# Forget gate's sums added on VectorE from a spread copy, in place of 8-row products on TensorE

## The reference

```
log_f = log_sigmoid(f_logit + forget_bias)            # (256, 8)
F = cumsum(log_f, axis=tokens)
logits[h,t,s] = q[t,h] . k[s,h] / 8 + F[t,h] - F[s,h]   # s <= t, else -inf
y_fox = softmax(logits) @ v
```

## Time and profile before

| | |
|---|---|
| median of 3 runs | 1119.39 us (1117.60 to 1119.49) |
| profiled execution | 1122.45 us, its span 1120.7 us |
| TensorE matmul busy | 1097.0 us, 98% |
| VectorE busy | 755.1 us, 67% |
| ScalarE busy | 604.4 us, 54% |
| GpSimd busy | 51.5 us, 5% |
| mean granted TensorE clock | 0.985 |
| DMA | 187.13 MB, 47.6% of the 16 engines' span for the weight queue |

### The profile page before, as it was taken

How to read it: one execution, slowest core, us unless ns; L and a number is a source line. 1 busy time by engine, 2 the same in 40 slices (tenths; PEclk the granted TensorE clock), 3 DMA queues, 4 the chain that set the end, 5 groups by cost and what they waited for, 6 DMA issues and landing times.

```text
span 1120.7 us, 22403 instructions
## 1 busy us (share of the span) xinstructions
PE 1097.0 (98%) x8864; PEld 1055.8 (94%) x8864; DVE 755.1 (67%) x1114; ACT 604.4 (54%) x898; POOL 51.5 (5%) x64
## 2 busy tenths in 40 slices
PE   8999999999999999999999999999997999999998
PEld 7899899899999999999999998988887999999998
DVE  6888897647776665567666677556657776665566
ACT  5447745486565454555555444545756565454453
POOL 0000000001310000110000010000000210000010
PEclk9999999999999999999999999989888999999999
DMA  6345434335545554565555455533323455555563
GB/s 243 114 160 170 150 118 151 113 113 188 180 170 214 187 189 165 185 212 188 200 198 177 160 200 190 174 128 113 113 76 113 163 186 216 187 187 175 185 213 113
DMA packets 31869, 187.13 MB, mean 167 GB/s; under 512 B 3904, under 2 KB 7360, under 8 KB 14016
## 3 DMA queue, kind: packets, MB, share of 16 engines
q1 hardware_dynamic: 31808, 186.27, 47.6%
HBM read 184.42 MB, written 1.05 MB: 166 GB/s over the span
## 4 chain that ended last, share of the span: by engine, by line
PE 89%; DVE 5%; ACT 3%; issue 2%; POOL 0%; DVEq 0%; POOLq 0%
PE acc L601 81%; PE area_a L601 4%; PE area_t L601 4%; DVE wlo L1440 1%; PE area_t L868 1%; ACT he L1089 1%; ACT L1089 0%; ACT s_z L1089 0%; DVE s_after L1992 0%; ACT s_a L1089 0%; ACT whi L1089 0%; DVE pp L1476 0%; DVE tmp L1618 0%; ACT n2r L1089 0%; ACT gates L1089 0%
## 5 line engine op out<-in xcount | busy, mean ns | idle before, releaser
L601 PE MATMUL acc<-hs,whi 128*128 128x256 f32 x3600 | 633.2, 280 | 3.5 <-DVE wlo L1440 2.0
L601 PEld LDWEIGHTS acc<-hs,whi 128*128 128x128 f32 x3600 | 551.1, 190 | 8.7 <-issue 5.8
L601 PE MATMUL acc<-hs,wlo 128*128 128x256 f32 x1800 | 502.1, 279 | 0.0
L1089 ACT ACTIVATE whi<-raw 128x1024 fp32r<-128x1024 f32 (+2 forms) x378 | 357.3, 981 | 162.1 <-PE acc L601 137.5
L1440 DVE TENSOR_TENSOR wlo<-raw,whi 128x1024 fp32r<-128x1024 f32 (+3 forms) x258 | 271.5, 1094 | 104.0 <-ACT whi L1089 103.3
L601 PEld LDWEIGHTS acc<-hs,wlo 128*128 128x128 f32 x1800 | 341.0, 189 | 0.2
L601 PE MATMUL acc<-hid,whi 128*128 128x256 f32 x1056 | 180.7, 277 | 0.2 <-DVE wlo L1440 0.2
L601 PEld LDWEIGHTS acc<-hid,whi 128*128 128x128 f32 x1056 | 159.1, 188 | 0.4 <-DVE wlo L1440 0.4
L601 PE MATMUL acc<-hid,wlo 128*128 128x256 f32 x528 | 146.0, 277 | 0.0
L1527 DVE TENSOR_TENSOR wlo<-raw,whi 128x1024 fp32r<-128x1024 f32 x120 | 141.2, 1219 | 6.3 <-ACT whi L1089 6.3
L1540 DVE TENSOR_TENSOR hbuf<-acc,sbuf 128x256 f32<-128x256 f32 x66 | 28.0, 425 | 113.8 <-PE acc L601 109.9
(11 more groups left out here) (315 smaller groups left out, 1071.9 us busy)
## 6 DMA issues: line engine op xcount, KB each, us to landing
raw<-in_w_gu SPq DMA_DIRECT2D x66, 1024.0 KB, 4.8
raw<-in_w_dn SPq DMA_DIRECT2D x48, 704.0 KB, 4.0
raw<-in_w_up SPq DMA_DIRECT2D x10, 1024.0 KB, 4.8
raw<-in_w_gates1b SPq DMA_DIRECT2D x8, 1024.0 KB, 4.8
raw<-in_w_out SPq DMA_DIRECT2D x8, 1024.0 KB, 4.8
raw<-in_w_qk SPq DMA_DIRECT2D x8, 1024.0 KB, 4.8
raw<-in_w_gates SPq DMA_DIRECT2D x8, 1024.0 KB, 4.8
raw<-in_w_projT_b SPq DMA_DIRECT2D x7, 1024.0 KB, 4.8
```

The source lines that it names most:

```text
L601: return nc.tensor.matmul(out, w, m, start=start, stop=stop, skip_group_check=True)
L1089: return nc.scalar.activation(out, in_, f, **kw)
```

## The change

`negf` becomes -F without the factor 8. TensorE's 8-row products in the fox_s steps are gone, and with them its wait for `forget_sums` and its use of `C_SEL` there. GpSimd gets a new part, `spread_forget`: it waits for `forget_sums`, stores `negf` to a DRAM scratch, waits for that, reads each head's row back to all 128 partitions with a DMA of its own (`decay_of`, in the order of the score slots), waits for all eight, and adds the causal mask in four instructions, one for each head group and query tile (`fox_bias`). VectorE waits for the one of these it needs (`fox_biased`) and adds `fox_bias` where it added the mask. `decay_of` lies where `osplit2_sb` comes later, `fox_bias` where `mixed2` and `up2` come later.

```
+        decay_of = arena("decay_of", 12288, (FOX_H, T))
+        fox_bias = [arena(f"fox_bias{tt}", 14336 + P * FOX_H * tt, (FOX_H, P * (tt + 1))) for tt in range(NT)]
...
-                        pe.wait_ge(S("forget_sums"), 1)
...
-                        m = mm(dst, q[cols(h), h // 2, queries(tt)], k[cols(h), h // 2, 0:keys(tt)], True, not fox)
-                        if fox:
-                            m = mm(dst, con[0:FOX_H, C_SEL + P * h:C_SEL + P * h + P], negf[0:FOX_H, 0:keys(tt)],
-                                   False, True)
+                        m = mm(dst, q[cols(h), h // 2, queries(tt)], k[cols(h), h // 2, 0:keys(tt)], True, True)
...
-                    v.tensor_scalar(negf[h, :], fsum[h, :], -float(HD) ** 0.5, None, ALU.mult)\
+                    v.tensor_scalar(negf[h, :], fsum[h, :], -1.0, None, ALU.mult)\
...
                     dve.wait_ge(S("a_full"), TURN_A[name] + 1)
+                    dve.wait_ge(S("fox_biased"), NT * hg + tt + 1)
                     v.scalar_tensor_tensor(f_sc[:, :, 0:ks], area_a[:, :, 0:ks], float(HD) ** -0.5,
-                                           heads4(causal(tt, C_CM), ks), ALU.mult, ALU.add)\
+                                           fox_bias[tt][:, 4 * hg:4 * hg + 4, :], ALU.mult, ALU.add)\
...
+            rows = nc.dram_tensor("forget_rows", (FOX_H, T), F32).ap()
+
+            def spread_forget():
+
+                pool.wait_ge(S("forget_sums"), 1)
+                pool.dma_start(rows, negf[0:FOX_H, :]).then_inc(S("forget_out"), 16)
+                pool.wait_ge(S("forget_out"), 16)
+                for n in range(FOX_H):
+                    h = n // 4 * 4 + HEAD_OF_SLOT[n % 4]
+                    pool.dma_start(decay_of[:, n, :], rows[h].partition_broadcast(P)).then_inc(S("forget_spread"), 16)
+                pool.wait_ge(S("forget_spread"), 16 * FOX_H)
+                for hg in range(2):
+                    for tt in range(NT):
+                        h, ks = slice(4 * hg, 4 * hg + 4), keys(tt)
+                        nc.gpsimd.tensor_tensor(fox_bias[tt][:, h, :], decay_of[:, h, 0:ks],
+                                                heads4(causal(tt, C_CM), ks), ALU.add).then_inc(S("fox_biased"), 1)
+
             gated_sums(up1, mixed1, BLOCKS["up1"], 24, 0)
             sum_squares(0)
             sum_squares(1)
             sum_squares(2)
+            spread_forget()
             gated_sums(up2, mixed2, BLOCKS["up2"], 16, 24)
```

## The result

| | before | after |
|---|---|---|
| median | 1117.69 us (5 runs, 1116.93 to 1119.49) | 1106.44 us (5 runs, 1104.61 to 1107.68) |
| ratio | | 0.9889, 95% interval 0.9876 to 0.9903 |
| profiled execution, span | 1122.45, 1120.7 us | 1105.72, 1103.9 us |
| mean granted clock | 0.985 | 0.995 |

The change makes the kernel about 1.1% faster: 11.3 us between these medians. The two profiled executions differ by more, 16.8 us of span; what follows has to explain both numbers.

The account below looks back on a forecast made before the run. TensorE bounds the kernel, with three engines handing each other work in the stage. Queue shifts of -16.5 us plus 0.3 and 1.0 gave -15.2, so 1104.2 us from the 1119.39 median; own range 1101.5 to 1107.5, wider 1101 to 1110.5.

Parts of the forecast that it names:

- 1, sb_s00: TensorE's fox_s00 shortens to 0.65 us and the tile behind it to 5.6, so sb_s00 is reached 5.9 us earlier.
- 4, stick-breaking 01: VectorE, no longer held at fox_s10, starts stick-breaking after sb_s01's logarithm, at 780.9 instead of 791.15: shift -10.3 us.
- 6, fox_s11's sum: VectorE's 3.37 us wait for TensorE before fox_s11's sum goes, bringing the accumulated shift to -13.6 us.
- 7, sb_s11's first pass: ScalarE's 2.88 us wait before sb_s11 goes; shift -16.5 us, kept by everything that follows.
- term (e): New TensorE gaps lower the clock behind them; only losses behind 790.5 count: 1.0 us added, bounds 0 and 3.0.
- the rival of the clock falling in the new gaps: Waits lower the clock behind sb_t01 and once more near fox_s10: saving only 11.5 us, time 1107.9; chance 12%.
- (d): Four GpSimd sums, 9 us in all at about 731 to 740, slow VectorE's splits: 0.3 us added, bounds 0 and 4.0.
- Term (a): VectorE's sum reads fox_bias instead of the mask, with same operands and shape: nothing added.
- Term (b): Scratch store and eight broadcasts after forget_sums at 714.7 land at 730 to 733, before first use at 746.8: nothing added.
- Term (c): Broadcasts share DMA engines with weight loads, which may land up to 4.8 us late: nothing added, bounds 0 and 2 us.
- Only the products' own time goes: In the fox_s steps, 64-row products stay slow and the clock still falls: perhaps 8 us saved, 1111; chance 4%.
- The late spread: GpSimd's DMAs run serially, fox_bias comes at 780, 33 us behind first use, stalling VectorE and TensorE: 1136; chance 5%.

Follow-up runs that it names:

- the second trace: Changed kernel run and profiled once more with no edit: 1106.31 us beside 1118.35 for the kernel before, ratio 0.990, span 1106.8.

## Why the prediction was right, and where it was off

The forecast was 1104.2 us and faster; the median is 1106.44, in the range of 1101 to 1110.5. The mechanism went step by step as forecast. The shifts compare the first two traces, each counted from its own fox_s00, which starts 0.8 us earlier after.

| step | forecast | measured |
|---|---|---|
| 1, sb_s00 (757.64, 751.17) | -5.9 | -5.7 |
| 2, fox_s01's sum (775.32, 767.73) | -6.9 | -6.8 |
| 3, sb_s01's first pass (784.07, 774.59) | -8.6 | -8.7 |
| 4, stick-breaking 01 (791.15, 780.00) | -10.3 | -10.4 |
| 6, fox_s11's sum (824.35, 811.34) | -13.6 | -12.3 |
| 7, sb_s11's first pass (834.21, 818.20) | -16.5 | -15.3 |
| sb_t11 (849.26, 833.23) | -16.5 | -15.3 |

The 1.2 us that steps 6 and 7 fall short are term (e): transposes of sb_t01 at 1.97 instead of 1.09 and the tile behind at 6.16.

**Step 1's size.** The saving was forecast as 15.2 us and is 11.3 in medians. That the time is only 2.2 us off is partly luck: the three runs of before that I started from had a median 1.7 us above that of the five. The mis-sized term is in the sum's basis. "The tile behind fox_s00 at 5.6 instead of 8.41" was read from one execution, and in the next the same tile took 5.79. I treated a fall of the clock at a certain place as part of the kernel, where only the falling somewhere is. That execution was also the dearest of all runs of before that I had, 3.06 above their median, and I subtracted the full saving from the median. Over all profiled executions the stage gained 13.2 us instead of 15.7 in the first pair; the medians give 11.3 and 12.0. A microsecond or so between 13.2 and these stays open, with three and two executions to take means from.

**Term (e), the new gaps**, 1.0 with bounds 0 and 3.0: 1.6 in the first trace after (0.9 for the transposes, 0.7 for the tile), 3.0 in the second, and none where the clock had fallen a tile sooner. The value was low, the bounds held, and the rival of the clock falling in the new gaps is partly true: the median lies between its 1107.9 and my 1104.2. In the second trace it came out at its upper bound. The grant there is 0.50 over the 1.97 us of the transposes and 0.73 over the 7.57 of the tile, by my working 6 us at 1.2 GHz, where more than 4 was a sign that the forecast is wrong; that execution took 1108.70 us. Another sign was missed by little, VectorE's wait of 0.61 us before fox_s10's sum where 0.5 was the most.

**The forecast's own range.** 1101.5 to 1107.5 does not follow from its reasons. With (d) and (e) at their bounds the sum is -16.5 to -9.5, so 1102.9 to 1109.9 us from the median of before, and 1 us more on each side. The median after lies in both.

**Term (a)**, nothing: right, the sums take 0.67 and 1.22 us as before. **Term (b)**, the spread: it landed 15.5 us behind `forget_sums` (713.23 to 728.74), where 730 to 733 behind 714.7 is 15.3 to 18.3 (14.0 in the second trace); the serial 64 was far off. The broadcasts took 6.5 us each in the median. The Trainium skill (DMA: Bandwidth & Descriptors, Anatomy of one DMA) gives 2.3 for one, and the estimate from it, landing by 721, was early by some 9 us; the measurement decides. **Term (c)**: ScalarE waited 1.78 us for a late weight load in the first trace after, 0.86 and 1.18 for two in the second, and TensorE for none. **Term (d)**: 0.3 forecast; 0 to 0.7 measured from `negf` to fox_s00, nothing in the times of the run with the spread alone. The mechanism was another than the sum had: I let a split grow by the ratio 0.24/0.43, but the two engines take turns. The pairs of splits were 1.08 and 0.49 us longer in the first trace after, the first pair 3.15 in the second (5.51 us), and it stayed off the path. The Trainium skill (SBUF — State Buffer, Who interferes with whom) has one block the other for whole instructions; the single instructions of the run with the spread alone agree, where each ends 1.08 to 2.24 us behind the end of the other engine's.

**The rivals.** "Only the products' own time goes" falls: the 64-row products did speed up. But its sister, which I did not write down, was the real alternative: the 8-row products need not go at all. The late spread did not come.

## What to carry to other kernels

When a short product is cheap on paper and its step is dear in the trace, compare the step with a like one without it, and then try the order before the removal: here four 64-row products followed by four 8-row ones gave all that a DRAM round trip and a third engine gave (1106.57 and 1106.44 us). Before a saving is subtracted, ask whether the part at the lower clock is the kernel's or that execution's, and take a second profile of the kernel before if there is one. Where a saving on TensorE ends in a wait, price the clock behind the wait; idle products bought it back at the one wait where they ended before the data came, and lost 1.8 us where they ended 2 us after it.

## What the runs showed of the hardware

Products on 8 rows that alternate with products on 64 rows take 3.31 us for 16 passes of 128 columns; grouped they take 1.73, at the same granted clock of 1.00. The clock fell from 2.4 to 1.2 GHz in or behind the alternated steps, behind waits of 4.24, 5.89 and 6.39 us and of 2.97 and 1.89, and in some executions in the tile behind fox_s10, after waits of 1.5 to 1.7 us; it fell neither at 64-row steps of 4.3 and 8.1 us nor behind the longest wait once idle products filled it but for 0.6 us. Where it falls differs between executions, and so does its price: the stage of the kernel before took 112.21 to 114.70 us. VectorE's splits and GpSimd's sums, both with two inputs in SBUF, ran by turns: a split of 1.2 us lasted 3.40 behind a sum of 2.41. GpSimd issued eight broadcasts of 128 KB in 4.28 us, about 0.54 each, and they landed 3.0 to 9.3 us after their issue.
